# A two-layer decoder step: samples taken out of the wide matrices, pages streamed beside them

## What is computed

```python
# layer 0
hp, hs = rms_norm(yp, g), rms_norm(ys, g)                  # D_MODEL = 1024
proj = h @ w_in                                            # 1024 x 4608
ro = head_group_norm(retention(rope(rq), rope(rk), rv, s0)) * silu(rg)    # s0: state of each sample
do = rms_norm(diff_attn(q, [k_past, k], [v_past, v]))      # past: 32 pages x 128 tokens per sample
y = y + concat(ro, do) @ w_out                             # 1536 x 1024
y = y + square(relu(rms_norm(y) @ w_up)) @ w_down          # 1024 x 4096 x 1024
# layer 1
u, v = split(gelu(rms_norm(y) @ w_in_odd))                 # 1024 x 6144
y = y + (u * (tril(w_s) . layer_norm(v) + b_s)) @ w_out_odd    # 3072 x 1024
y = y + square(relu(rms_norm(y) @ w_up)) @ w_down
```

## Time and profile before

| | us |
|---|---|
| median of 3 runs | 2046.82 (2042.52 to 2046.92) |
| the profiled execution | 2045.41 |
| its span, first to last instruction | 2043.6 |
| PE busy | 1882.8 (92%) |
| DVE busy | 909.9 (45%) |
| ACT busy | 568.6 (28%) |
| POOL busy | 636.0 (31%) |

### The profile page before, as it was taken

How to read it: one execution, slowest core, us unless ns; L and a number is a source line. 1 busy time by engine, 2 the same in 40 slices (tenths; PEclk the granted TensorE clock), 3 DMA queues, 4 the chain that set the end, 5 groups by cost and what they waited for, 6 DMA issues and landing times.

```text
span 2043.6 us, 35465 instructions
## 1 busy us (share of the span) xinstructions
PE 1882.8 (92%) x14237; PEld 1683.9 (82%) x14237; DVE 909.9 (45%) x1155; ACT 568.6 (28%) x915; POOL 636.0 (31%) x510
## 2 busy tenths in 40 slices
PE   4967888899998799999999999979999999999998
PEld 4855555555554599999999899879999999999997
DVE  2577676665552544332333423393323443323331
ACT  4422333322231232221222232303313333212221
POOL 1388554777740013300431100023304224102400
PEclk8988898999996799999999999979999999999999
DMA  6258686899997223332323322202322232332221
GB/s 206 92 165 270 232 258 207 315 335 356 337 320 243 94 83 94 99 92 90 92 93 93 95 63 82 67 10 74 101 86 92 89 98 83 104 91 86 92 93 63
DMA packets 218268, 287.95 MB, mean 141 GB/s; under 512 B 12977, under 2 KB 149762, under 8 KB 217858
## 3 DMA queue, kind: packets, MB, share of 16 engines
q1 hardware_dynamic: 215306, 281.95, 41.8%
q10 hardware_dynamic: 2208, 2.75, 0.4%
q0 software_dynamic: 624, 1.44, 0.4%
HBM read 274.89 MB, written 11.21 MB: 140 GB/s over the span
## 4 chain that ended last, share of the span: by engine, by line
PE 81%; DVE 8%; DMA 3%; ACT 3%; SPq 2%; issue 2%; POOL 1%; ACTq 0%; DVEq 0%
PE ps L1639 18%; PE ps L1641 18%; PE ps L1640 18%; PE ps L1449 6%; PE ps L1451 5%; PE ps L1450 5%; PE ps L1495 4%; DMA vbuf<-in_cache_v 2%; DVE Sc L1138 1%; PE ps L1540 1%; POOL kbuf L633 1%; PE ps L1706 1%; PE ps L1422 1%; PE ps L1527 1%; PE ps L1519 1%
## 5 line engine op out<-in xcount | busy, mean ns | idle before, releaser
L488 DVE TENSOR_TENSOR w_lo<-raw,w_hi 128x1024 fp32r<-128x1024 f32 x238 | 334.7, 1414 | 498.2 <-ACT w_hi L481 497.1
L1639 PE MATMUL ps<-xg_hi,w_hi 128*128 128x260 f32 x1408 | 398.6, 283 | 0.5 <-DVE sTs L1409 0.5
L1641 PE MATMUL ps<-xg_hi,w_lo 128*128 128x260 f32 x1408 | 398.4, 283 | 0.0
L1640 PE MATMUL ps<-xg_lo,w_hi 128*128 128x260 f32 x1408 | 397.3, 282 | 0.0
L633 POOL TENSOR_TENSOR kbuf<-kbuf,Qb 128x512 f32<-128x512 f32 x256 | 344.4, 1373 | 141.0 <-DMA kbuf<-in_cache_k 140.9
L481 ACT ACTIVATE w_hi<-raw 128x1024 fp32r<-128x1024 f32 x248 | 259.1, 1054 | 460.9 <-PE ps L1641 413.0
L1449 PE MATMUL ps<-w_hi,xg_hi 128*128 128x256 f32 (+1 forms) x1200 | 352.4, 294 | 21.8 <-DVE w_lo L488 9.4
L1450 PE MATMUL ps<-w_lo,xg_hi 128*128 128x256 f32 (+1 forms) x1200 | 344.6, 287 | 0.0
L1451 PE MATMUL ps<-w_hi,xg_lo 128*128 128x256 f32 (+1 forms) x1200 | 344.2, 287 | 0.0
L1641 PE MATMUL ps<-h_hi,w_lo 128*128 128x260 f32 x1024 | 289.3, 283 | 0.0
L1639 PE MATMUL ps<-h_hi,w_hi 128*128 128x260 f32 x1024 | 289.1, 282 | 0.0
(11 more groups left out here) (274 smaller groups left out, 2543.0 us busy)
## 6 DMA issues: line engine op xcount, KB each, us to landing
kbuf<-in_cache_k SPq DMA_DIRECT2D x256, 256.0 KB, 4.5
vbuf<-in_cache_v SPq DMA_DIRECT2D x256, 256.0 KB, 4.9
raw<-in_w_ffn_up SPq DMA_DIRECT2D x64, 512.0 KB, 3.8
raw<-in_w_ffn_down SPq DMA_DIRECT2D x64, 512.0 KB, 3.5
raw<-in_w_in_odd SPq DMA_DIRECT2D x48, 512.0 KB, 3.8
raw<-in_w_in_even SPq DMA_DIRECT2D x36, 512.0 KB, 5.5
raw<-in_w_out_odd SPq DMA_DIRECT2D x24, 512.0 KB, 3.6
raw<-in_w_out_even SPq DMA_DIRECT2D x12, 512.0 KB, 3.6
```

Source lines behind the costliest of these rows:

```text
L488: dve.tensor_tensor(w_lo[:, c.slot], raw[:, c.slot % 2], w_hi[:, c.slot].bitcast(F32), ALU.subtract).then_inc(lo_made, 1)
L1639: pe.matmul(out, wh, xh, start=kk == 0, stop=False, skip_group_check=True)
L1640: pe.matmul(out, wh, xl, start=False, stop=False, skip_group_check=True)
L1641: mm_ = pe.matmul(out, wl, xh, start=False, stop=kk == KC * groups - 1, skip_group_check=True)
```

## The change

The samples leave the wide products and the v half. `wide` is kept for the second MLP alone; the other wide phases use `prompts`, with the 512 prompt tokens as one operand of 512 columns in one PSUM bank and 24 matmuls per chunk. The samples' own products run in plain fp32 behind the prompts: SP loads the 148 chunks of oe, up, dn, v, u and oo of these layers again, unsplit, into a `ring` of four buffers, and PE multiplies each by the 8 samples in four matmuls of 256 columns, each in its own column group ("sW"). After a pair of macros ACT copies the sum ("sE"), PE folds the groups and turns the result to columns ("sF"), and DVE and ACT apply residual, norm, squared relu, gelu or gate. At the second MLP the samples' columns are put beside the prompts' again ("sM3").

The written-out order now covers 276 slots: 90 tiles of "in", 8 tail slots, one slot per chunk of oe, up0, dn0, u and oo, one per tile of v, and 6 in the gate stage. `PACE` says how many ticks (stream steps, then sample steps) a slot gets. This puts, by count, K pages: 128 in the tiles of "in", 12 in the tail, 28 beside oe, 40 beside up00, 40 beside dn00 and 8 beside up01; V pages: 84, 12, 28, 40, 40, 40 and 12 beside dn01; sample chunks: 4 beside dn01, 38 beside v, 18 in the gate stage, 18 beside u0, 27 beside oo0, 27 beside u1, 16 beside oo1, none beside u2 and oo2.

Further: the sample tile goes first in every macro, and those of macros 0 and 1 before any prompt tile; weights 2 and 3 load into buffers of their own in the prologue, between the halves of x; DVE makes all low parts; the samples' states are worked off head by head between the tiles of "in", in pairs of samples ("sL", "sM", "sU", "sO"); u and oo are cut in three thirds instead of two halves; the loops of all phases but the second MLP are unrolled; most buffers have new places. In POOL's and ACT's programs the slot's background steps come ahead of the halves of the macro before.

```diff
-            + [("v", 2, N_V)] + [(f"{k}{h}", g, m) for h in range(2) for k, g, m in (("u", 2, 6), ("oo", 3, 4))]
+            + [("v", 2, N_V)] + [(f"{k}{h}", g, m) for h in range(3) for k, g, m in (("u", 2, 4), ("oo", 2, 4))]
...
-LAG = SPS + 4
+LAG = SPS + 6
...
+def _tiles():
+    seq = [(0, NT), (1, NT)]
+    for m in range(N_IN):
+        seq += [(m, NT)] * (m > 1) + [(m, t) for t in range(NT)]
+    return seq
...
+    pace, after = 0.0, []
+    for j in range(slots):
+        kind = "in" if j < NTILE + TAIL else SLOT_KIND[j - NTILE - TAIL]
+        if j >= FIRST_STEP:
+            pace += PACE[kind]
+        now = []
+        while pace >= 1.0 and ticks:
+            now.append(ticks.pop(0))
+            pace -= 1.0
+        if j < NTILE + TAIL:
+            now = first[j] + (now[0] if now else []) + middle[j] + [s for tick in now[1:] for s in tick] + late[j]
+        else:
+            now = [s for tick in now for s in tick]
+        after.append(now)
+    assert not ticks, len(ticks)
...
+def gemms():
+    out, first = [], 0
+    for name, groups, pairs in (("oe", 3, 2), ("up", 2, 8), ("dn", 8, 2), ("v", 2, 6), ("u", 2, 6), ("oo", 6, 2)):
+        for q in range(pairs):
+            out.append((name, q, [(first + i, i // groups, i % groups, groups) for i in range(2 * groups)]))
+            first += 2 * groups
+    return out
+GEMM = gemms()
+LOADS = [(name, q, mm, g) for name, q, chunks in GEMM for _, mm, g, _ in chunks]
...
+    for p, (name, q, chunks) in enumerate(GEMM):
+        for n, *_ in chunks:
+            tick([("sW", n)])
+        ticks[-1].append(("sE", p))
+        later(2, ("sF", p))
+        if name == "u":
...
+SLOT_KIND = (["oe"] * 12 + ["up"] * 16 + ["dn"] * 16 + ["up"] * 16 + ["dn"] * 16 + ["v"] * (NT * N_V) + ["gate"] * 6
+             + ["u"] * 48)
...
+PACE = {"in": 0.75, "oe": 1.2, "up": 1.2, "dn": 1.3, "v": 1.0, "gate": 3.0, "u": 3.4}
...
+            def ring_in(n):
+                if n < len(LOADS):
+                    name, q, mm, g = LOADS[n]
+                    w, at = sample_weights[name]
+                    wait(sp, s_multiplied, n + 1 - RING)
+                    sp.dma_start(ring[:, n % RING], chunk_rows(w, g, at + CW * (2 * q + mm))).then_inc(ring_loaded[n % RING], 16)
...
+            def expand(name, make, hh, ll):
+                c0, groups, macros = PHASES[name]
+                for m in range(macros):
+                    for g in range(groups):
+                        background(slot_of(c0 + groups * m + g))
+                        if g == 0 and m > 0:
+                            halves_of(name, m - 1, make, hh, ll)
+                halves_of(name, macros - 1, make, hh, ll)
...
+                    else:
+                        pe.wait_ge(s_done, g + 1 + (8 if name == "oo" else 0))
+                        src = hsT if name == "dn" else gsT
+                    pe.wait_ge(ring_loaded[i % RING], 16 * (i // RING + 1))
+                    for k in range(KC):
+                        row = (P // QUAD) * k
+                        last = pe.matmul(ps[row:row + NS, PV[p % 2], CW * mm:CW * mm + CW], src[:, KC * g + k, :],
+                                         ring[:, i % RING, k, :], start=g == 0, stop=g == last_group, skip_group_check=True)
+                    last.then_inc(s_multiplied, 1)
+                elif kind == "sF":
+                    pe.wait_ge(s_copied, i + 1)
+                    wait(pe, out_read, OUT_FILL[step])
+                    for b in range(4):
+                        last = pe.matmul(ps[:, OUT, NS * b:NS * b + NS], osb[:, P * b:P * b + P], C["fold"], start=True, stop=True)
...
+            def prompts(name, high, low, ready, counts, e=None):
+                c0, groups, macros = PHASES[name]
+                for m in range(macros):
+                    wait(pe, acc_read, BLOCK0[name] + 2 * m - 2)
+                    for g in range(groups):
+                        c = Chunk(0, 0, 0, c0 + groups * m + g)
+                        pe.wait_ge(lo_made, c.n + 1)
+                        pe.wait_ge(ready, counts[g])
+                        for blk in range(2):
+                            out, cols = sums(m, blk), slice(P * blk, P * blk + P)
+                            for k in range(KC):
+                                kk = KC * g + k
+                                wh, wl, xh, xl = w_hi[:, c.slot, k, cols], w_lo[:, c.slot, k, cols], high(kk), low(kk)
+                                pe.matmul(out, wh, xh, start=kk == 0, stop=False, skip_group_check=True)
+                                pe.matmul(out, wh, xl, start=False, stop=False, skip_group_check=True)
+                                last = pe.matmul(out, wl, xh, start=False, stop=kk == KC * groups - 1, skip_group_check=True)
+                        last.then_inc(chunk_multiplied, 1)
+                        if e is not None and m == 0 and g == 0:
+                            squares(e)
+                        background(slot_of(c.n))
```

More of the change, by code:

```diff
@@ L123, in plan @@
[L123 to L132, removed]
+    slots = NTILE + TAIL + len(SLOT_KIND)
+    first, middle, late = ([[] for _ in range(slots)] for _ in range(3))
@@ L175, in constants @@
+assert any(("f2",) in now for now in AFTER[:V0])
 def constants():
@@ new lines, in load, with slots_of @@
+            def load(n):
+                name = [k for k, (c0, groups, macros) in PHASES.items() if c0 <= n < c0 + groups * macros][0]
+                m, g = divmod(n - PHASES[name][0], PHASES[name][1])
+                chunk_in(Chunk(0, 0, 0, n), weights(name), g, CW * m)
+            def slots_of(name):
+                c0, groups, macros = PHASES[name]
+                for c in range(c0, c0 + groups * macros):
+                    load(c + AHEAD + 1)
+                    for step in AFTER[slot_of(c)]:
+                        sp_step(step)
@@ L584, in step, with stream @@
+            def stream(name, per, begin=0):
+                c0, groups, macros = PHASES[name]
+                w = weights(name)
                 def step(i):
@@ L1322, in project, with expand_loop @@
[L1322 to L1325 removed]
+                repeat(dve, macros // 2, step, first=macros // 2 if name == "dn11" else 1)
+            def expand_loop(name, e=None):
                 c0, groups, macros = PHASES[name]
@@ L1608, in _, with background @@
-            pe.wait_ge(f_squared, 1)
-            pe.matmul(ps[:, TURN, 128:160], ones[:, :], fr, start=True, stop=True, skip_group_check=True).then_inc(f_ss, 1)
-            pe.wait_ge(so_done, 1)
-            pe.wait_ge(out_read, len(OUT_FILL))
-            for b in range(8):
-                last = turn(ps[:, OUT, NS * b:NS * b + NS], sro[:, P * b:P * b + P], NS)
-            last.then_inc(mix_ready, 1)
-            pe.wait_ge(mix_lo, 14)
-            def wide(name, per, src_hi, src_lo, ready, counts, e=None, first=1):
+            def background(j):
+                for step in AFTER[j]:
+                    pe_step(step)
@@ new lines, in _ @@
+            pe.wait_ge(gate_loaded, 16 * 5)
+            pe.wait_ge(nat_read, NTILE + NT * N_V)
+            for g in range(8):
+                last = turn(ps[:, 4 + g // 4, P * (g % 4):P * (g % 4) + P], wsr[:, g, :], P)
+            last.then_inc(ws_turned, 1)
+            pe.wait_ge(ws_masked, 1)
+            for g in range(8):
+                last = pe.matmul(ps[:, g // 4, P * (g % 4):P * (g % 4) + P], ones[:, :], wsT[:, g, :],
+                                 start=True, stop=True, skip_group_check=True)
```

1623 lines of the change are left out of this document (993 added, 630 removed).

## The result

The changed kernel takes 2023.74 us (median of 7 runs, 2018.75 to 2031.68); the kernel before took 2042.06 us in the same session (7 runs, 2039.19 to 2046.92). The ratio of after to before is 0.991, 95% interval 0.989 to 0.993. The forecast of 1927 us (range 1840 to 2010) had the sign right and the size wrong by 97 us. The profiled execution of the changed kernel took 2023.74 us, span 2021.8.

The account below looks back on a forecast made before the run. Pages were taken to limit the input stage, with DMA idling afterwards. Terms 28.9 + 440 + 24 + 480 + 169 + 50 + 345 + 387.6 gave a 1924.5 us span, hence 1927 us forecast (range 1840 to 2010).

Parts of the forecast that it names:

- PE's own work in the input stage: Input stage: TensorE's busy work, 248 for tiles, 20 for V pages and 115 for everything else, sum 383 us.
- The density: Input stage: share of the time TensorE is busy, taken as 0.87, making 440 us; bounds 412 and 505 us.
- Natural tiles: Input stage: 88 tiles of 24 matmuls of 256 columns at 2.82 us each, 248 us of TensorE work.
- The rest: Input stage: TensorE's differential attention, retention, transposes and states, 185 us by difference, taken as 115 (bounds 80 and 185).
- Rival 2: Input stage: DVE and ACT chains keep it at density 0.76, 505 us, +65, whole 1992 us; chance 0.22.
- Prologue: Before the input stage: no change, the 88 tiles start at 28.9 us as now; bounds -5 and +6.
- Tail: End of the input stage: the old 64 us shrink to the 12 mix transposes, 24 us.
- Oe and first MLP: Output projection and first MLP: 444.4 to 480 us, with 405 for 76 chunks, 39 V bursts, 16 late pages.
- Samples beside v, gate, u and oo: Stages with sample chunks at 0.55 us each: v half 169, gate 50, u and oo 345 us.
- Rival 3: Sample chunks: PE stands in order behind each ring chunk, 148 x 1.5 = +222, whole 2149 us; chance 0.11.
- the first (denser): Whole kernel: input stage at 0.93, wide matmul at its floor, no stalls, 1838 us; chance 0.18.
- the fourth: Whole kernel: the change does not move the limit, 2045 us, stream costing PE what the first stage loses; chance 0.02.

Follow-up runs that it names:

- filler run: Changed kernel plus 128 useless matmuls run by PE in eight attention units before it waits for the exponentials: 2020.18 us, 0.990 of the kernel before.
- adjacent-score run: Changed kernel with each unit's two score matmuls next to each other, then its two mask matmuls: 2001.83 us, 0.980 of the kernel before.
- early-exponential run: Changed kernel with the exponential step one slot earlier in 8 of the 16 attention units: 1994.39 us, 0.978 of the kernel before.
- prologue run: Changed kernel, each half of x loaded ahead of two weight chunks, sample tiles evacuated before the prompts' squares: 2021.72 us, 0.990 of the kernel before.

## Why the prediction was wrong

**The failed step is PE's own work in the input stage**, "88 x 2.82 = 248 ... I take 115 ... Sum 383 us". It was 434. The density that the forecast put on it, 0.87, came out: 434 / 504.9 = 0.86. In part that is luck, for the forecast had PE held by a VectorE busy 0.73 of the stage, and it was 0.55. The forecast guarded the density with bounds and two rivals, and the work with nothing but the wide bounds of its last term.

- *Natural tiles, 248 against 283.* 2.82 us is the price of a tile at the full clock. The stage ran at 0.90 before (0.92 up to 640 us, without its tail) and runs at 0.90 now. 285 matmuls at 0.213 us instead of 0.118 are 27 of the 35 us; most of the rest stands in first matmuls behind another kind of work. I charged the waits in the density and the clock nowhere, although it was in the same row, and expected without saying so that fewer page waits would restore it. The trace of the kernel before had the answer: between 28.9 and 640 us the natural matmuls of its 90 tiles, counted start to start, take 280.7 us, 3.12 a tile, and 216 of them are cold. Their high x high third, before and (L1872, above) now, has a mean of 300 and of 308 ns, where one at the full clock lasts 0.28 us:

```profile
L1449 PE MATMUL ps<-w_hi,xg_hi 128*128 128x256 f32 (+1 forms) x720 | 216.3, 300 | 17.7 <-DVE w_lo L488 9.4 <-ACT stg L789 4.3 <-ACT dvn L789 3.9
```

  Fewer page waits did not restore the clock. By the trace, some 80 of the 285 cold matmuls come behind waits for exponentials (10.1 us of such waits before, 16.1 now); the filler run shows the link for these. Some 60 come behind waits of the samples' states, which the change moved between these tiles, 38 in the first 15 us, and others behind waits of rotation, retention and mixing; that idle time is the cause there too is likely, but not shown. The pages have a share: without them 221 are left and the natural tiles take 276 us.
- *The rest, 115 against 127.* "Cleared of waits" was too generous: the masks between the scores cost them their overlap (14 us, shown by the adjacent-score run), and at the lower clock these fp32 matmuls too take longer (8 us in the early-exponential run). The same count of the trace before gives 120 us between 28.9 and 640 and 31 for the states behind; the forecast's 185 was a difference from natural tiles at 2.82.
- *V, 20 against 23*: right.

**Rival 2** named the right time for this stage (505 us) with chains of DVE and ACT and the pages as the reason. Half shown: without pages the stage is still 446.8 us, so of 505 us the pages hold 58, 23 of them V matmuls. It was not VectorE's load (0.55 busy, where the forecast set 0.8 as the sign): of PE's idle time 16.1 us are waits for exponentials, 15.0 the one wait behind the rotation and some 15 waits for the mix, its copies and its values.

**Prologue, 0 against +10.** The text gave +6 as the bound. x was late behind weights, and PE's third tile waited for ACT to evacuate the first sample tile (6.7 us), queued behind the squares for the norm. By the prologue run, where the prompts start at 34.5 us, this costs the whole next to nothing.

**Tail, 24 against 33.7.** DVE is busy 27.1 of these 33.7 us: with 12 K sums in the tail the mix's low parts wait for it; without pages it takes 28.4, so the pages explain half of the 10 us, and the other half is open.

**Oe and first MLP, 480 against 490.** The 1824 products take 433 us, start to start, for 405: 18 us by the spacing (0.232 for 0.222) and 10 us in the products next to each burst and macro, at 0.31 to 0.43 us. V bursts at 0.97 us and five spreads and folds as forecast; the 16 us for late pages did not come (PE waits for no page and is idle 4.1 us in all). So the 10 us missed are +28 on the products and about -18 on waits and transitions.

**Samples beside v, gate, u and oo** were right as a sum (564 us forecast, 569.8 measured) and in their price: one chunk takes 0.50 us beside u and oo and 0.55 beside v, for 0.55. In u and oo errors cancelled, which is luck: the products take 276 us for 256, the waits 12 for 20 and the sample chunks 44 for 48. Rival 3 did not come: PE's waits for the ring are 7.0 us in u and oo. **The other rivals**: of the first (denser) only the missing stalls came, not the density nor the floor of the wide matmul; nothing of the fourth came; the stream's slack did pay for the re-read weights, but of the 119 us expected to be left over, 22 were.

## What to carry to other kernels

Price an operation at the clock of its own stage: if the row says 0.90, either multiply or name the wait that will go and show that it is the one ahead of the cold matmuls. The trace of the stage before has that price: divide the time of all its tiles by their number, not that of one undisturbed tile. PE waits of 2 to 4 us cost nearly twice their length here (31 us of stage for 15.2 us of wait), so short ping-pong waits in a mixed stage can be worth more than their sum. Look for half-height matmuls with a full-height one between them: putting them side by side took 18.5 us off the stage here, as much as the whole change gained.

## What the runs showed of the chip that I had not expected

- Two fp32 matmuls on different row halves and banks overlap fully when adjacent (0.84 us for both, 0.84 for one) and not at all with a 128-row matmul between (0.84 us each).
- 128 useless matmuls in the waits cut the cold natural matmuls from 285 to 213 and did not slow the kernel (2020.18 against 2023.74 us).
- Products of 512 columns are 0.232 us apart in the median, those of 256 columns 0.118: 19 ns and 11 ns over the columns at 2.4 GHz (213.3 and 106.7). The Trainium skill ("TensorE: Matmul & The Clock Gate", Back-to-back issue gap) has 2.5 ns over them for what it calls the isolated gap; in this kernel, with its weight loads of 128 columns between, the trace does not agree, and the measured spacing decides.
